# Taking the seven ones-matmuls out of each of the six sandwich norms of a five-block language model kernel

## The reference

```python
def rms_norm(t, g, eps=NORM_EPS):
    t32 = t32 * lax.rsqrt(jnp.mean(t32 * t32, axis=-1, keepdims=True) + eps)
    return t32.astype(t.dtype) * g.astype(t.dtype)
...
        f = swiglu(rms_norm(h, ln_ffn1[i, 0]), ffn1_w_gu[i], ffn1_w_down[i])
        h = h + 0.5 * rms_norm(f, ln_ffn1[i, 1])
        hn = rms_norm(h, ln_mix[i, 0])
...
        h = h + rms_norm(m, ln_mix[i, 1])
        f = swiglu(rms_norm(h, ln_ffn2[i, 0]), ffn2_w_gu[i], ffn2_w_down[i])
        h = h + 0.5 * rms_norm(f, ln_ffn2[i, 1])
```

## Time and profile before

| | |
|---|---|
| median of 3 runs | 1453.66 us (1453.46 to 1454.67) |
| the profiled execution | 1454.77 us, span of the trace 1453.0 us |
| PE busy | 1402.9 us, 97% of the span |
| PEld busy | 1361.8 us, 94% |
| DVE busy | 896.7 us, 62% |
| ACT busy | 653.5 us, 45% |
| mean granted TensorE clock | 0.992 of full speed |
| HBM read | 225.44 MB, 156 GB/s over the span |

### The profile page before, as it was taken

The page is one execution under the profiler, slowest core; times in us unless marked ns, Lnnn a source line. Parts: engine busy times, 40 slices in busy tenths (PEclk is TensorE's granted clock), DMA queues, the critical chain, the costliest instruction groups (busy, mean ns, idle before and its releaser), DMA issues.

```text
span 1453.0 us, 26632 instructions
## 1 busy us (share of the span) xinstructions
PE 1402.9 (97%) x10924; PEld 1361.8 (94%) x10924; DVE 896.7 (62%) x1329; ACT 653.5 (45%) x925; POOL 12.5 (1%) x26
## 2 busy tenths in 40 slices
PE   6999999999999999999999999999999997999997
PEld 6999999998999999999998988999998986899997
DVE  4666547657666537666457877666546566577543
ACT  5444435345444435444444555544535425444332
POOL 0000000000000000000000000000001100000000
PEclk9999999999999999999999999999999999999999
DMA  6555543343555433555553223455653411355550
GB/s 241 174 173 206 199 173 131 131 135 126 173 174 205 174 142 117 173 173 210 181 183 112 82 84 117 167 181 192 231 184 127 175 59 59 125 194 180 196 175 30
DMA packets 29353, 227.54 MB, mean 157 GB/s; under 512 B 3376, under 2 KB 4672, under 8 KB 5088
## 3 DMA queue, kind: packets, MB, share of 16 engines
q1 hardware_dynamic: 28656, 224.75, 44.0%
q0 software_dynamic: 624, 1.77, 0.3%
HBM read 225.44 MB, written 1.06 MB: 156 GB/s over the span
## 4 chain that ended last, share of the span: by engine, by line
PE 84%; DVE 10%; ACT 4%; issue 2%; DMA 0%; DVEq 0%; ACTq 0%
PE ps L1370 24%; PE ps L1372 24%; PE ps L1371 24%; DVE w_lo L813 4%; PE ps L1384 2%; ACT w_hi L446 2%; PE ps L1436 2%; PE ps L1395 1%; PE ps L1396 1%; PE ps L1400 1%; ACT s_exp L594 1%; DVE small L1009 0%; PE ps L1576 0%; PE ps L1578 0%; PE ps L1577 0%
## 5 line engine op out<-in xcount | busy, mean ns | idle before, releaser
L813 DVE TENSOR_TENSOR w_lo<-w_raw,w_hi 128x2048 fp32r<-128x2048 f32 (+2 forms) x188 | 482.0, 2564 | 232.7 <-ACT w_hi L446 232.7
L1370 PE MATMUL ps<-x_hi,w_hi 128*128 128x272 f32 (+1 forms) x2136 | 616.1, 288 | 5.9 <-DVE w_lo L813 5.7
L1372 PE MATMUL ps<-x_hi,w_lo 128*128 128x272 f32 (+1 forms) x2136 | 612.5, 287 | 0.0
L1371 PE MATMUL ps<-x_lo,w_hi 128*128 128x272 f32 (+1 forms) x2136 | 610.7, 286 | 0.0
L446 ACT ACTIVATE w_hi<-w_raw 128x2048 fp32r<-128x2048 f32 (+2 forms) x188 | 401.1, 2134 | 425.9 <-PE ps L1372 420.1
L1370 PEld LDWEIGHTS ps<-x_hi,w_hi 128*128 128x128 f32 x2136 | 403.8, 189 | 13.4 <-DVE w_lo L813 7.2
L1372 PEld LDWEIGHTS ps<-x_hi,w_lo 128*128 128x128 f32 x2136 | 403.9, 189 | 0.0
L1371 PEld LDWEIGHTS ps<-x_lo,w_hi 128*128 128x128 f32 x2136 | 403.5, 189 | 0.3 <-issue 0.2
L1370 PE MATMUL ps<-hid_hi,w_hi 128*128 128x272 f32 (+1 forms) x960 | 276.1, 288 | 0.2 <-DVE w_lo L813 0.2
L1372 PE MATMUL ps<-hid_hi,w_lo 128*128 128x272 f32 (+1 forms) x960 | 274.8, 286 | 0.0
L1371 PE MATMUL ps<-hid_lo,w_hi 128*128 128x272 f32 (+1 forms) x960 | 273.7, 285 | 0.0
(11 more groups left out here) (264 smaller groups left out, 1229.3 us busy)
## 6 DMA issues: line engine op xcount, KB each, us to landing
w_raw<-w_gu SPq DMA_DIRECT2D x88, 1024.0 KB, 4.9
w_raw<-w_dn SPq DMA_DIRECT2D x32, 1408.0 KB, 6.0
w_raw<-w_ff SPq DMA_DIRECT2D x32, 1024.0 KB, 4.9
w_raw<-w_conv_in SPq DMA_DIRECT2D x8, 1536.0 KB, 6.6
w_raw<-w_qkv SPq DMA_DIRECT2D x8, 1536.0 KB, 6.6
w_raw<-w_mix_in SPq DMA_DIRECT2D x8, 1536.0 KB, 6.5
w_raw<-w_conv_out SPq DMA_DIRECT2D x4, 1024.0 KB, 4.8
w_raw<-w_attn_out SPq DMA_DIRECT2D x4, 1024.0 KB, 5.0
```

The costliest lines, as they stand in the source:

```text
L813: dve.tensor_tensor(w_lo[j % SPLIT][:, 0:width], w_raw[j][:, 0:width], w_hi[j % SPLIT][:, 0:width].bitcast(F32), ALU.subtract).then_inc(lo ...
L1370: pe.matmul(out_ap, w_hi[slot][:, cols], hi(k), start=first, stop=False)
L1371: pe.matmul(out_ap, w_hi[slot][:, cols], lo(k), start=False, stop=False)
L1372: mm = pe.matmul(out_ap, w_lo[slot][:, cols], hi(k), start=False, stop=last)
```

## The change

The helper `keep_warm` and its only call are taken out. The seven matmuls are gone in each of the six seams, and with them the wait for the constants' load, which had long been over. No other instruction is added, moved or changed.

```diff
@@ -1429,12 +1429,6 @@
 
                 loop(pe, DN_N, step)
 
-            def keep_warm(count):
-
-                pe.wait_ge(consts_loaded, 16)
-                for _ in range(count):
-                    pe.matmul(ps[:, 5, 0:3 * P], ones[:, :], sq3[:, :], start=True, stop=True)
-
             def sum_squares(u, c0):
 
 
@@ -1445,7 +1439,6 @@
                 last = square[(KD - 1) % 2]
                 pe.matmul(ps[:, SUM + 1, c0:T], ones[:, :], last[:, c0:T], start=False, stop=True).then_inc(sumsq_summed_act, 1)
                 pe.matmul(ps[:, SUM, c0:T], ones[:, :], last[:, c0:T], start=False, stop=True).then_inc(sumsq_summed_dve, 1)
-                keep_warm(7)
 
             def convolution(q):
                 n0 = FIRST["conv_in"]
```

## The result

| | changed | before |
|---|---|---|
| median | 1465.87 us (1461.57 to 1467.69, 7 runs) | 1454.67 us (1453.46 to 1457.69, 7 runs) |
| profiled execution | 1466.99 us, span 1465.2 | 1454.77 us, span 1453.0 |
| mean granted TensorE clock, profiled execution | 0.980 | 0.992 |

The ratio is 1.0071, with a 95% interval from 1.0059 to 1.0083: slower by 11.2 us by the medians, where +5.2 us was predicted and 1462.2 us was the upper end of the range. The direction was right and the size was not. A later set of four runs of the same kernel gave 1462.7 us against 1454.64, a ratio of 1.0052 (1.0034 to 1.0070); the two sets together put the loss at 8 to 11 us. The profiled execution is one of the slower ones of its seven.

What follows compares the result with a forecast made beforehand. PE's matmul stream was taken to bound the kernel. An earlier start (-3.6), slow-clock loss (+8.0) and double stretches (+0.8) summed to +5.2 us, giving 1458.9 us, 0.36% slower; range for 8 in 10, 1454.6 to 1462.2.

Steps and rivals of the forecast that it cites:

- What bounds the kernel, and the gap: PE's matmul stream sets the time nearly everywhere; the change leaves PE idle 3.8 us at five seams, 4.8 at the fifth.
- I take it that the clock falls at all six: At the six seams, each new PE gap brings the granted clock from 2.4 to 1.2 GHz.
- What a microsecond at 1.2 GHz costs: In the seams' first blocks, each microsecond PE works at the lower clock loses 0.46; 8.0 us over six seams.
- How long it stays down: After a fall at a seam the clock stays low 3.4 us, of which PE works 2.95 on average, 2.53 at the fifth.
- A double stretch: At a seam with an early fall the clock stays down 6.8 us, 1.57 us more; one in every second execution, 0.8 us.
- Earlier start: PE starts the first block sooner: 0.70 us at four seams, 0.78 at the sixth, none at the fifth; 3.6 us gained.
- the first block of conv_in: Sign: conv_in's first block ends about 0.7 us later than before, counted from the last sum of squares.
- the mean clock: Sign: the granted clock's mean over the span drops from 0.992 to about 0.985.
- the clock did not hold: Rival: the clock stays up through the seams' gaps, leaving only the earlier start, 1450.5 us; chance 0.08.
- Nothing was absorbed: Rival: only some seams fall, or waits behind them, as for w_lo, absorb the loss; 1454 to 1455.5 us; chance 0.11.
- More than one stretch at most seams: Rival: gaps keep the clock down twice at three or more seams, 1463 us; chance 0.04.
- The rest: Elsewhere, existing stretches at 1.2 GHz may fall differently once everything is shifted: 1.5 us either way.

Runs made afterwards that it cites:

- fill0: Kernel before with three of its own gaps filled by ones-matmuls and none at the six seams; 1462.67 us, ratio 1.0052 to the kernel before.
- w6: Six ones-matmuls instead of seven at each seam of the kernel before; 1455.82 us, ratio 1.0000.
- w4: Four ones-matmuls instead of seven at each seam of the kernel before; 1454.13 us, ratio 0.9999.
- best: Kernel before with three of its own gaps filled, six ones-matmuls at five seams and seven at the fifth; 1451.20 us, ratio 0.9973.
- fill: Kernel before with three of its own gaps filled and seven ones-matmuls kept at each seam; 1452.56 us, ratio 0.9987.
- hold: Changed kernel with PE waiting at each seam for x_hi of tile 1 instead of tile 0; 1468.48 us, ratio 1.0093 to the kernel before.
- w2: Two ones-matmuls instead of seven at each seam of the kernel before; 1459.17 us, ratio 1.0027.

## Why the prediction was right and wrong

*What bounds the kernel, and the gap:* right. The two waits quoted from the profile aren't all that PE has (there is one of 10.0 us at the program's start, and shorter ones in the heads and the last block), but none of the others lies between a seam's sums and its first block. The gaps are 3.83 us (predicted 3.8) and 4.79 at the fifth (4.8), and what is lost on PE at a seam is paid: fill0's seam ends and its time agree.

*"I take it that the clock falls at all six":* right, in both traces of the changed kernel and in fill0, 18 of 18.

*"What a microsecond at 1.2 GHz costs", 0.46:* right. The fourth seam lost 2.33 + 0.45 = 2.78 us against the same seam without a fall, while PE worked 6.05 us of the stretch: 0.46. In the second trace 1.05 + 0.45 = 1.50 over 3.26 us worked: 0.46 as well. The Trainium skill (TensorE: Matmul & The Clock Gate, Terms) takes half of all the time at the lower clock, an estimate of 3.4 and 1.7 us here; the measured pair stays below it, also when only the time that PE worked is halved (3.0 and 1.6).

*"How long it stays down", and "A double stretch":* this is the step that failed. I let the fall come anywhere from 1.7 us ahead of the restart to 1.3 behind, and counted an early fall as the cheap one, because a part of its 3.4 us would pass while PE is idle (0.8 us at the least), with a double stretch once in two executions. The 38 falls at seams show the reverse: a fall that comes 0.78 us or more ahead of the restart is the dear one, since the clock then stays down for 6.8 us. The changed kernel had three and two double stretches in its two traces, fill0 three. The cheap single stretch wasn't seen: with a fall around the restart nearly all of the 3.4 us is worked. It costs 1.3 to 1.6 us each, 1.53 on average over the seven in the two traces (seam ends less the earlier start), and not the mean of 1.36. In sizes: six single stretches at 1.53 make 9.2 us where 8.0 stood. A double one costs 2.4 to 2.8 us, about 1.03 more and not the 1.57 that I took, and there are eight in the three traces, 2.7 in each: 2.8 where 0.8 stood. The row of the long stretch in the earlier trace rows already showed PE idling in it, 6.31 us busy of 6.90, while through the stretches behind 310.34 and 1252.42 PE worked without a pause; I gave it a chance instead of a condition.

*"Earlier start", 3.6 us:* mis-sized. It measures 2.1 us by the seam ends of w6, w4 and best, because the matmul that came out of the wait took 0.33 us in the chain where the one in the stream took 0.13, and because x_lo of tile 0 isn't there yet at the two-part blocks. The first I left out; the second I had named for one rival only.

With the three terms as measured the sum is -2.1 + 9.2 + 2.8 = +9.9 us, against 10.1 between fill0 and fill, and 8.1 and 11.2 in the two sets of the changed kernel. It is 4.7 above the predicted 5.2: 2.0 of that are double stretches, 1.2 single ones and 1.5 the earlier start. So the sign was not luck, but the three errors all went one way. The terms were read from the traces after the fact, and only their sum is tested by a time. Of the signs that were named, the first block of conv_in ended 1.10 us later in the first trace and 1.14 in the second, where about 0.7 stood, and the mean clock was 0.980 and 0.984, where about 0.985 stood.

*The rivals:* the clock did not hold. Nothing was absorbed: PE's waits for w_lo are 7.9 us in nine places as before. "More than one stretch at most seams", given 0.04, was the nearest to what happened, at half of the seams.

*"The rest", 1.5 us either way:* the spread of the kernel before itself, 1452.1 to 1458.0 us, is larger than this. The stretch near 875 us in the first trace stands at the gap of 1.45 us in the attention heads that the change doesn't touch.

What stays open is what else than the gap's length decides on a fall for gaps between about 1.4 and 3.1 us: with the same program the clock fell at some seams and not at others. Why a stretch is double stays open too. That PE was still idle 0.78 us or more after the fall goes together with it in all 38 cases at the seams, but not elsewhere (w6 near 868 us, the kernel before near 1205). No run varied that idle time alone, and hold, which was to do it, did not settle it.

## What to carry to other kernels

Filler matmuls in a forced gap of PE pay when the gap brings the clock down, and they needn't fill it: here four to seven served alike, and two, one or one in the middle did not. With six, which end when x_hi arrives, and three other gaps filled, the kernel was at its fastest. Where an operand ends the gap anyway, its price is not its idle time but what comes behind it, here 1.5 us for a fall near the restart and 2.4 to 2.8 us when PE is still idle 0.8 us after the fall. When you price a fall of the clock from a trace, go by the longest stretch as well as by the usual one and ask what PE was doing in it; and compare the ends of matmuls, not their starts, when one of them comes out of a wait.

## What the runs showed of the hardware that was not expected

- A stretch at 1.2 GHz lasted 3.4 us or 6.8 us at every seam, and which of the two went with PE's restart in all 38 falls there: up to 0.43 us after the fall, short; 0.78 us or later, long. Elsewhere one of 6.8 us had PE back 0.31 us after the fall (w6, 867.55 us), and one lasted 17.07 us (w2, 1209.97 us).
- Two gaps of 1.54 and 1.39 us with 0.91 us of matmuls between them brought the clock down at two of the four seams of that form, though the single gap of 1.46 us in the earlier trace rows had not. A single one of 1.45 us in the attention heads did in the changed kernel and in w6, and 1.46 us in the same place did not in the kernel before. The Trainium skill's limit of about 3 us for a gap (TensorE: Matmul & The Clock Gate, Why this matters for your kernels) is too wide for this kernel.
- The same program varied by 5.8 us over 26 runs on one chip (1452.14 to 1457.96 us), and the mean granted clock went with it, from 0.995 to 0.990.
